# Modulation loaded in two column halves, three layer-1 products split along their rows, memory loaded first

## The chip, the cores and the metric

The kernel runs on one core of one Trainium2 chip. TensorE (PE in the rows) multiplies matrices, VectorE (DVE), ScalarE (ACT) and GpSimd (POOL) work element by element, and SyncE (SP) issues most of the transfers from HBM into SBUF. The metric is the device time of one execution in microseconds, the median of several runs. Lower is better.

## What is computed

Three layers over 256 tokens of width 2048, all in float32. Layer 1, cut to what the change touches:

```
mod = silu(c) @ w_ada + b_ada                       # w_ada: 2048 x 6144
shift, scale, gate = split(mod, 3)
h = rms_norm(x, norm_gain) * (1 + scale) + shift
q_sb, k_sb, v_sb, z_sb, q_r, k_r, v_r, z_r = split(h @ w_in, 8)
oa = stick_breaking_attention(rms_norm(q_sb), rms_norm(k_sb), v_sb) * silu(z_sb)
ob = head_group_norm(retention(rotary(q_r), rotary(k_r), v_r)) * silu(z_r)
x  = x + gate * (concat(oa, ob) @ w_out)
```

Layers 2 and 3 attend, among much else, to a memory of 256 rows: `mem_n = rms_norm(mem)`, and `mem_n @ w_mk`, `mem_n @ w_mv` for each of the two layers. These four memory products depend on nothing of layer 1.

## The kernel before, in words

**Products.** Each product with a weight is a `Gemm`. Its weight comes in chunks of 512 KB (128 partitions x 1024 numbers) into the ring `raw` of `SLOTS` = 6 slots. ScalarE rounds a chunk to `w_hi` (`split_hi`, L364), VectorE computes the rest `w_lo` (`split_lo`, L368), which lies in the same bytes as `raw`, and TensorE multiplies with both (L431 and L432, or L425 to L427 where tokens are the rows of the result). The inputs are kept as a high and a low part too (`xA`). SP issues the load of chunk n once TensorE has used up chunk n - 6 (`chunk_used`, L360). ScalarE and VectorE walk through the chunks with `run_split`: at step i they split chunk i + 3 (`AHEAD` = 3), and before and behind the split they run the small steps of whatever else is under way ("hooks" at positions p, two to a chunk; an odd p comes behind the split). Every engine works through its own list in the order in which it is written; nothing is reordered.

**Order of the products.** `G_MEM` (32 chunks: the four memory products), then `G_SBQK` (q_sb, k_sb, 32 chunks), `G_SBV` (16), `G_RTQK` (32), `G_RTV` (16), `G_SBZ` (16), `G_RTZ` (16), `G_OUT`. The attention of the stick-breaking heads runs in the hooks of `G_RTQK` (`sb_hook`, four units of 8 chunks), the retention in those of `G_SBZ` and `G_RTZ` (`rt_hook`, four units of 8 chunks).

**Modulation.** `silu(c) @ w_ada` is computed on VectorE: GpSimd loads 1 MB pieces of `w_ada` (128 rows of one third) into `ada_ring` (4 slots, L518), VectorE multiplies each by its scalar and adds it to `ada_sum` (L1062), and TensorE adds up the partitions at the end (`ada_columns`, L1629). The 32 pieces of shift and scale are used up during the memory norm and `G_MEM`, the 16 of gate during `G_SBQK` and `G_SBV`, one in four and one in two chunks.

**The start.** SP issues `vec`, `con`, `memT` (2 MB), `xT` (2 MB), and then weights; GpSimd issues the first pieces of `w_ada` beside them. ScalarE squares the memory (L579), TensorE adds the squares over the features (L1615), ScalarE forms the inverse root (L597, L600), and VectorE and ScalarE normalise 16 tiles (L1003, L606, L1009) with `ada` pieces in between. Behind `G_MEM` stand the columns of shift and scale, and then norm 1 of all 16 tiles of x; `G_SBQK` starts with the first four tiles.

## Time and profile before

| | us |
|---|---|
| median of 3 runs (1883.63 to 1887.93) | 1885.12 |
| the profiled execution | 1890.45 |
| its span, first to last instruction | 1888.6 |
| TensorE busy in the span | 1784.2 (94%) |
| VectorE busy | 1235.9 (65%) |
| ScalarE busy | 902.7 (48%) |

In the rows below, a product instruction's line says which kind it is, "idle before <-releaser" says how long the engine had been idle and what ended it, and PEclk is the granted TensorE clock (1.00 is 2.4 GHz, 0.5 is 1.2 GHz). A stage's end is read from the first instruction of the next one.

### The profile page before, as it was taken

To read this page: it belongs to the slowest core of one execution; us is meant where nothing else is said; L and a number is where in the kernel's file an instruction comes from. 1 tells how busy PE (TensorE), PEld (TensorE's weight loads), DVE (VectorE), ACT (ScalarE), POOL (GpSimd) and SP (SyncE) were. 2 spreads that over 40 slices of the span, in tenths; PEclk is the share of its full clock that TensorE was granted. 3 is DMA by queue.
4 is the path that set the end of the run, shared out by engine and by line. 5 is a ranking of instruction groups with operands and counts; after the bars stand their busy time and mean duration, and the time that the engine had idled before them with its cause. 6 is when DMAs were issued, how large, how long until landed. Compare 5 with 4: busy or idle time off the path is not lost.

```text
span 1888.6 us, 23572 instructions
## 1 busy us (share of the span) xinstructions
PE 1784.2 (94%) x9703; PEld 1517.6 (80%) x9703; DVE 1235.9 (65%) x1520; ACT 902.7 (48%) x1158; POOL 75.7 (4%) x87
## 2 busy tenths in 40 slices
PE   1699999999999989999999999999989999999897
PEld 1577888888887878888888888788878888878786
DVE  3978767655477655788567766865464667566754
ACT  2333544454356434666344565644354555455632
POOL 0111000000000000011000000000000000000010
PEclk9798999999999999999999999999989999999999
DMA  8897888556444546666654555565546565444463
GB/s 304 328 350 294 296 290 298 153 148 177 135 145 141 190 149 169 188 189 180 178 145 138 153 167 162 167 191 185 187 141 178 162 194 146 123 123 123 134 187 115
DMA packets 304874, 350.51 MB, mean 186 GB/s; under 512 B 10416, under 2 KB 286000, under 8 KB 298624
## 3 DMA queue, kind: packets, MB, share of 16 engines
q1 hardware_dynamic: 297744, 298.34, 52.5%
q0 software_dynamic: 7024, 50.66, 6.9%
q8 instruction: 78, 1.28, 0.3%
q14 instruction: 28, 0.23, 0.0%
HBM read 346.87 MB, written 2.10 MB: 185 GB/s over the span
## 4 chain that ended last, share of the span: by engine, by line
PE 90%; DVE 5%; DMA 2%; ACT 2%; issue 2%; SPq 0%; DVEq 0%
PE psG L431 48%; PE psG L432 24%; PE psG L425 3%; PE psG L426 3%; PE psG L427 3%; DVE ada_sum L1062 1%; DMA P<-in_memT 1%; PE psH L1615 1%; DMA raw<-in_mem_w 1%; PE psH L1604 1%; DVE w_lo L368 1%; PE psH L1629 1%; DVE W L1003 1%; ACT w_hi L364 1%; PE psH L1890 1%
## 5 line engine op out<-in xcount | busy, mean ns | idle before, releaser
L431 PE MATMUL psG<-xA,w_hi 128*128 128x512 f32 x3520 | 1281.8, 407 | 53.4 <-issue 24.4
L432 PE MATMUL psG<-xA,w_lo 128*128 128x256 f32 x3520 | 994.7, 283 | 0.0
L368 DVE TENSOR_TENSOR w_lo<-raw,w_hi 128x1024 fp32r<-128x1024 f32 (+1 forms) x560 | 686.5, 1239 | 356.9 <-ACT w_hi L364 355.4
L431 PEld LDWEIGHTS psG<-xA,w_hi 128*128 128x128 f32 x3520 | 670.0, 190 | 226.5 <-issue 50.1
L364 ACT ACTIVATE w_hi<-raw 128x1024 fp32r<-128x1024 f32 (+1 forms) x560 | 572.9, 1045 | 372.2 <-DMA raw<-in_w_out 163.9
L432 PEld LDWEIGHTS psG<-xA,w_lo 128*128 128x128 f32 x3520 | 673.7, 191 | 4.4 <-issue 3.8
L400 ACT ACTIVATE P<-psG 128x512 f32<-128x512 f32 x102 | 60.6, 594 | 217.5 <-PE psG L432 217.4
L1033 DVE TENSOR_TENSOR P<-psG,P 128x512 f32<-128x512 f32 (+2 forms) x103 | 70.4, 683 | 116.4 <-ACT P L400 114.1
L1062 DVE SCALAR_TENSOR_TENSOR ada_sum<-ada_ring,silc,ada_sum 128x2048 f32<-128x2048 f32 x48 | 112.6, 2347 | 3.9 <-DMA ada_ring<-in_w_ada 3.8
L425 PE MATMUL psG<-w_hi,xA 128*128 128x512 f32 x192 | 77.7, 405 | 4.4 <-DVE memkv L1033 3.9
L426 PE MATMUL psG<-w_lo,xA 128*128 128x512 f32 x192 | 76.9, 400 | 0.0
L427 PE MATMUL psG<-w_hi,xA 128*128 128x512 f32 x192 | 76.7, 399 | 0.0
L431 PE MATMUL psG<-xB,w_hi 128*128 128x512 f32 x192 | 67.7, 395 | 0.0
L1615 PE MATMUL psH<-W,con 128*128 128x256 f32 x74 | 21.7, 436 | 35.4 <-ACT W L579 35.4
L432 PE MATMUL psG<-xB,w_lo 128*128 128x256 f32 x192 | 53.8, 280 | 0.0
L544 POOL TENSOR_TENSOR W<-W 128x512 f32<-128x512 f32 x9 | 12.5, 1385 | 1007.8 <-ACT W L579 1007.8
L1040 DVE TENSOR_TENSOR xT<-psG,xT 128x512 f32<-128x512 f32 x32 | 22.1, 692 | 45.1 <-PE psG L432 44.6
L431 PE MATMUL psG<-xQ,w_hi 128*128 128x512 f32 x144 | 50.9, 399 | 0.0
L425 PEld LDWEIGHTS psG<-w_hi,xA 128*128 128x128 f32 x192 | 37.5, 195 | 13.3 <-DVE memkv L1033 4.3
L431 PE MATMUL psG<-xK,w_hi 128*128 128x512 f32 x128 | 47.0, 406 | 0.0
L1615 PEld LDWEIGHTS psH<-W,con 128*128 128x128 f32 x74 | 15.3, 220 | 39.0 <-issue 28.5
L427 PEld LDWEIGHTS psG<-w_hi,xA 128*128 128x128 f32 x192 | 37.3, 194 | 8.1
(291 smaller groups left out, 1492.0 us busy)
## 6 DMA issues: line engine op xcount, KB each, us to landing
raw<-in_w_in SPq DMA_DIRECT2D x360, 512.0 KB, 3.8
raw<-in_w_out SPq DMA_DIRECT2D x128, 512.0 KB, 3.4
ada_ring<-in_w_ada POOLq DMA_DIRECT2D x48, 1024.0 KB, 7.9
raw<-in_mem_w SPq DMA_DIRECT2D x32, 512.0 KB, 9.3
raw<-in_w_uq SPq DMA_DIRECT2D x24, 384.0 KB, 3.3
raw<-in_w_ukv SPq DMA_DIRECT2D x32, 128.0 KB, 2.4
raw<-in_w_ukv SPq DMA_DIRECT2D x16, 256.0 KB, 3.2
P<-in_memT SPq DMA_DIRECT2D x1, 2048.0 KB, 25.6
```

Source lines behind the costliest of these rows:

```text
L364: nc.scalar.activation(slot(w_hi, n), slot(raw, n), ACT.Copy).then_inc(hi_ready, 1)
L368: nc.vector.tensor_tensor(slot(w_lo, n), slot(raw, n), slot(w_hi, n), ALU.subtract).then_inc(lo_ready, 1)
L400: nc.scalar.activation(g.dst(b), product(g, b, 0), ACT.Copy).then_inc(copied, 1)
L425: nc.tensor.matmul(out, x_hi, hi[:, w], start=first, stop=False)
L426: nc.tensor.matmul(out, x_hi, lo[:, w], start=False, stop=False)
L427: last = nc.tensor.matmul(out, x_lo, hi[:, w], start=False, stop=end)
L431: nc.tensor.matmul(psG[:, bank + f, :], hi[:, w], x, start=first, stop=False)
L432: last = nc.tensor.matmul(psG[:, bank + f, S:2 * S], lo[:, w], x[:, 0:S], start=False, stop=end)
L1033: v.tensor_tensor(g.dst(b), product(g, b, 1), g.dst(b), ALU.add).then_inc(features_landed, 1)
L1040: ins = v.tensor_tensor(x, src, x, ALU.add)
L1062: v.scalar_tensor_tensor(out=ada_sum[:, part, :], in0=ada_ring[:, n % ADA_SLOTS, :], scalar=silc[:, k:k + 1], in1=ada_sum[:, part, :], op0 ...
L1615: ins = mm(psH[:, norm_bank(n), 0:S], ones, norm_squares(n, g)[:, j * S:j * S + S], start=g == 0 and j == 0, stop=g == 3 and j == 3)
```

## The change

**Memory first.** `memT` comes in four parts of 512 KB, ahead of `con`; `xT` is issued behind the first eight weight chunks; GpSimd issues no `w_ada` before it has pre-added the squares of the memory (`add_squares(0)`: of three groups in four TensorE then has one matmul instead of four, and of norm 1 likewise).

**Modulation in halves.** Shift and scale are loaded as 512 KB pieces (128 rows, half of a third's columns) into a ring of six slots. The 32 pieces of the first column half are used up in `G_MEM`, the 32 of the second in a new stage. Norm 1 of tiles 0 to 7 needs the first half alone and runs in the last three steps of `G_MEM`; tiles 8 to 15 follow in the last three steps of the new stage.

**Products in two halves.** `G_SBQK0`, `G_RTQK0` and `G_SBV0` (16 + 16 + 8 chunks, the new stage of 40) multiply with the first 1024 rows of the weights, which needs tiles 0 to 7. `G_SBQK`, `G_SBV` and `G_RTQK` then do the other 1024 rows (16 + 8 + 16 chunks) and VectorE adds them to what stands in `P` (`adds`: two instructions of 128x512 for each block of two chunks, L1109). `G_RTQK` now spans two units of `sb_hook`; the other two run in `G_RTV`.

**Gate in the weight ring.** The 32 half pieces of the gate are loaded by SP into `raw` itself, as items between the weights (`ITEMS`): behind every second chunk of `G_SBQK`, `G_SBV`, `G_RTV` and `G_SBZ`, and behind every fourth of `G_RTQK`. Item j takes the slot of item j - 6. The piece behind chunk i is added on VectorE at step i, behind the split of chunk i + 3. The gate's columns on TensorE come in two halves, behind `G_RTQK` and behind `G_SBZ`.

```diff
-ADA_SUM, ADA_RING, FIRST_CON, FIRST_WORK = 16, 32, 64, 72
-ADA_SLOTS = 4
-ADA_FIRST, ADA_BLOCK = 8, 6
-SHIFT_AT = 11
+MEM_RAW, FIRST_CON, FIRST_WORK = 32, 64, 72
+ADA_SUM, ADA_RING, GATE_SUM = 64, (48, 52, 56, 60, 72, 76), 60
+ADA_HALF = 32
+MEM_UNITS, EARLY_UNITS = 32, 40
...
+        self.adds, self.per = adds, per or kt // 2
+        self.copied, self.by_scalar = not adds and bool(dst), not adds and bool(tokens)
...
+        def early(k0):
+
+            return dict(x=lambda k: xA[:, k0 + k, :], ready=lambda tiles: (q["nm_lo"], 16 + k0 + tiles), adds=k0 > 0, per=8)
...
-        G_SBQK = Gemm(KT, 8, columns(w_in, 0), dst=into(SBQ), pair=True, **h1)
-        G_SBV = Gemm(KT, 2, columns(w_in, 2048, 512, 2), cols=512, kk=2, tokens=copy_tokens(SBV), **h1)
-        G_RTQK = Gemm(KT, 8, columns(w_in, 4096), dst=into(RTQ), **h1)
+        G_SBQK0, G_SBQK = (Gemm(8, 8, columns(w_in, 0, row0=k0 * NP), dst=into(SBQ), pair=True, **early(k0)) for k0 in (0, 8))
+        G_RTQK0, G_RTQK = (Gemm(8, 8, columns(w_in, 4096, row0=k0 * NP), dst=into(RTQ), **early(k0)) for k0 in (0, 8))
+        G_SBV0, G_SBV = (Gemm(8, 2, columns(w_in, 2048, 512, 2, row0=k0 * NP), cols=512, kk=2, tokens=copy_tokens(SBV),
+                              **early(k0)) for k0 in (0, 8))
...
-        ORDER = [*G_MEM, G_SBQK, G_SBV, G_RTQK, G_RTV, G_SBZ, G_RTZ, G_OUT,
+        ORDER = [*G_MEM, G_SBQK0, G_RTQK0, G_SBV0, G_SBQK, G_SBV, G_RTQK, G_RTV, G_SBZ, G_RTZ, G_OUT,
...
+        GATE_AT = {G_SBQK: lambda i: i % 2 == 1, G_SBV: lambda i: i % 2 == 1, G_RTQK: lambda i: i % 4 == 3,
+                   G_RTV: lambda i: i % 2 == 1, G_SBZ: lambda i: i % 2 == 1}
+        ITEMS = []
+        for g in ORDER:
+            for i in range(len(g.order)):
+                ITEMS.append(("weight", g.c0 + i))
+                if g in GATE_AT and GATE_AT[g](i):
+                    ITEMS.append(("gate", sum(kind == "gate" for kind, _ in ITEMS)))
+        PLACE, LOADS = {}, []
+        for j, (kind, n) in enumerate(ITEMS):
+            by_tile = kind == "weight" and CHUNKS[n][0].by_tile
+            LOADS.append((LOADS[j - SLOTS] if j >= SLOTS else 0) + (CHUNKS[n][0].kk if by_tile else 1))
+            PLACE[kind, n] = j
+
+        def arrived(eng, kind, n):
+            j = PLACE[kind, n]
+            eng.wait_ge(raw_loaded[j % SLOTS], 16 * LOADS[j])
 
         def landed(eng, g, blocks=None):
...
+            j = PLACE["weight", g.c0]
+            end = PLACE["weight", g.c0 + len(g.order)] if g is not ORDER[-1] else len(ITEMS)
+            for j in range(j, end):
+                kind, n = ITEMS[j]
+                if j >= SLOTS:
+                    before, m = ITEMS[j - SLOTS]
+                    sp.wait_ge(*((chunk_used, m + 1) if before == "weight" else (ada_used, 2 * ADA_HALF + m + 1)))
+                if kind == "gate":
+                    k, half = m_to_gate(n)
+                    sp.dma_start(raw[:, j % SLOTS, :], ada_rows(k, 2, half)).then_inc(raw_loaded[j % SLOTS], 16)
+                    continue
+                _, b, c = CHUNKS[n]
+                src, out = g.src(b, c), low(n, raw).rearrange("p (k n) -> p k n", k=g.kk)
                 if g.by_tile:
                     for k in range(g.kk):
-                        sp.dma_start(out[:, k, :].rearrange("p (h n) -> p h n", n=NP), src[:, k]).then_inc(raw_loaded[n % SLOTS], 16)
+                        sp.dma_start(out[:, k, :].rearrange("p (h n) -> p h n", n=NP), src[:, k]).then_inc(raw_loaded[j % SLOTS], 16)
                 else:
-                    sp.dma_start(out, src).then_inc(raw_loaded[n % SLOTS], 16)
...
+            for g in range(4):
+                sp.dma_start(mem_raw[:, 4 * g:4 * g + 4, :], io["memT"].rearrange("(t p) s -> p t s", p=NP)[:, 4 * g:4 * g + 4, :])\
+                  .then_inc(mem_loaded[g], 16)
...
+                if g is G_MEM[0]:
+                    sp.dma_start(xT[:, :, :], io["xT"].rearrange("(t p) s -> p t s", p=NP)).then_inc(loaded["x"], 16)
                 if g is G_SBQK:
-                    sp.wait_ge(q["nm_ss"], 8)
+                    sp.wait_ge(q["ada_cols"], 2)
...
+            add_squares(0)
+            for m, (half, k, part) in enumerate(ADA_ORDER):
+                slot = m % len(ADA_RING)
+                if m == 20:
+                    add_squares(1)
+                if m >= len(ADA_RING):
+                    pool.wait_ge(ada_used, m + 1 - len(ADA_RING))
...
+                if unit in (6, 8, 11, 13):
+                    act.wait_ge(loaded["x"], 16)
+                    norm_square(1, (6, 8, 11, 13).index(unit), xT)
+                if unit == 18:
+                    norm_inverse_root(1)
+                if unit >= MEM_UNITS - 3:
...
+                if g.tokens:
+                    out, bank = g.tokens(b), set_of(g, b)
+                    v.tensor_tensor(out, psG[:, bank:bank + 2, :], out, ALU.add).then_inc(vector_landed, 1)
...
+                    n = m - 2 * ADA_HALF
+                    k, half = m_to_gate(n)
+                    arrived(dve, "gate", n)
+                    src, out = raw[:, PLACE["gate", n] % SLOTS, :], gate_sum[:, :]
+                    if k == 0 and half:
+                        dve.wait_ge(q["gate_cols"], 1)
+                if k == 0:
+                    v.tensor_scalar(out, src, silc[:, k:k + 1], None, ALU.mult).then_inc(ada_used, 1)
+                else:
+                    dve.wait_ge(ada_used, m - (m < 2 * ADA_HALF))
+                    v.scalar_tensor_tensor(out=out, in0=src, scalar=silc[:, k:k + 1], in1=out, op0=ALU.mult,
+                                           op1=ALU.add).then_inc(ada_used, 1)
...
+            def half_norm(half, step):
+                if step == 0:
+                    modulation(half)
+                    dve.wait_ge(q["nm_rs"], 2)
+                for t in (range(0, 4), range(4, 7), range(7, 10))[step]:
+                    norm_step(1, xT, gs, mod, 8 * half + t, 8 * half, 8 * half + 8)
...
+                        for m in range(done[u], done[u + 1]):
+                            ada_add(ADA_HALF * half + m)
+                        if u >= units - 3:
+                            half_norm(half, u - (units - 3))
...
+            def gate_hook(g, u0=0):
+
+                def hook(b, p):
+                    i = 8 * b + p // 2
+                    if p % 2 and GATE_AT[g](i):
+                        ada_add(2 * ADA_HALF + ITEMS[PLACE["weight", g.c0 + i] + 1][1])
+                return hook
+
...
+            def modulation_columns(half):
+                pe.wait_ge(ada_used, ADA_HALF * (half + 1))
+                ada_columns(ada_sum[:, 0, :], 8 * half, None)
+                ada_columns(ada_sum[:, 1, :], KT + 8 * half, "ada_cols", first=False)
+
+            def gate_columns(half):
+                pe.wait_ge(ada_used, 2 * ADA_HALF + KT * (half + 1))
+                ada_columns(gate_sum[:, :], 32 + 8 * half, "gate_cols")
...
+            pe.wait_ge(q["sb_y"], 2)
+            gate_columns(0)
+            run_products(pe, G_RTV, lambda b, p: sb_hook(2 + b, p))
```

How SP's list stands in the stage of `G_SBV`; `raw` is the ring, `in_w_in` the weights, `in_w_ada` the gate's pieces. Before, where `con_65` are constants of layer 1:

```order
L360 DMA raw<-in_w_in 128x4x256 [waits chunk_used] x32
L505 DMA con_65<-in_con 128x1672 [waits nm_ss]
L360 DMA raw<-in_w_in 128x2x512 [waits chunk_used] x16
L360 DMA raw<-in_w_in 128x4x256 [waits chunk_used] x32
L360 DMA raw<-in_w_in 128x2x512 [waits chunk_used] x16
```

and now, from the second half of `G_SBQK` into that of `G_SBV`:

```order
L394 DMA raw<-in_w_in 128x4x256 [waits chunk_used] x2
L386 DMA raw<-in_w_ada 128x1024 [waits ada_used]
L551 DMA con_72<-in_con 128x1672 [waits ada_cols]
L394 DMA raw<-in_w_in 128x2x512 [waits chunk_used] x2
L386 DMA raw<-in_w_ada 128x1024 [waits ada_used]
L394 DMA raw<-in_w_in 128x2x512 [waits chunk_used] x2
L386 DMA raw<-in_w_ada 128x1024 [waits ada_used]
```

What moved: between each two weight loads stands a load that waits for VectorE's addition of an earlier gate piece.

How VectorE's list stands at the start of `G_SBQK`. Before:

```order
L368 TENSOR_TENSOR w_lo<-raw,w_hi 128x1024 x4
L1062 SCALAR_TENSOR_TENSOR ada_sum<-ada_ring,silc,ada_sum 128x2048
L368 TENSOR_TENSOR w_lo<-raw,w_hi 128x1024 x3
L1033 TENSOR_TENSOR P<-psG,P 128x512
L368 TENSOR_TENSOR w_lo<-raw,w_hi 128x1024
L1062 SCALAR_TENSOR_TENSOR ada_sum<-ada_ring,silc,ada_sum 128x2048
```

and now, in its second half:

```order
L409 TENSOR_TENSOR w_lo<-raw,w_hi 128x1024
L1145 SCALAR_TENSOR_TENSOR gate_sum<-raw,silc,gate_sum 128x1024
L1109 TENSOR_TENSOR P<-psG,P 128x512 x2
L409 TENSOR_TENSOR w_lo<-raw,w_hi 128x1024 x2
L1145 SCALAR_TENSOR_TENSOR gate_sum<-raw,silc,gate_sum 128x1024
L1109 TENSOR_TENSOR P<-psG,P 128x512 x2
```

What moved: an addition of a gate piece stands behind every second split instead of every fourth, and each pair of splits is followed by two additions of products. VectorE's list in `G_MEM`, before:

```order
L368 TENSOR_TENSOR w_lo<-raw,w_hi 128x1024
L1062 SCALAR_TENSOR_TENSOR ada_sum<-ada_ring,silc,ada_sum 128x2048
L368 TENSOR_TENSOR w_lo<-raw,w_hi 128x1024
L1062 SCALAR_TENSOR_TENSOR ada_sum<-ada_ring,silc,ada_sum 128x2048
```

and now:

```order
L409 TENSOR_TENSOR w_lo<-raw,w_hi 128x1024
L1145 SCALAR_TENSOR_TENSOR ada_sum<-ada_ring_70,silc,ada_sum 128x1024
L409 TENSOR_TENSOR w_lo<-raw,w_hi 128x1024
L1145 SCALAR_TENSOR_TENSOR ada_sum<-ada_ring_71,silc,ada_sum 128x1024
```

What moved: each split is followed by half as large a piece.

## Rows read from the trace of the kernel before

**Rows 1.** The page, 40 slices of the span: busy tenths of TensorE

```profile
PE   1699999999999989999999999999989999999897
```

**Rows 2.** Windows: window, length, busy us (instructions) of PE, PEld, DVE, ACT, POOL, PEclk, DMA share, GB/s

```profile
49.60:110.00 60.40, 47.03 (x200) 39.15 (x200) 54.52 (x50) 23.20 (x31) 7.44 (x15) 0.81 0.90 334
110.00:181.30 71.30, 68.26 (x346) 57.55 (x344) 58.52 (x40) 22.81 (x24) 6.08 (x12) 0.95 0.90 336
...
278.00:321.60 43.60, 43.60 (x195) 36.09 (x194) 35.81 (x25) 18.52 (x18) 2.64 (x5) 1.00 0.90 313
321.60:437.00 115.40, 115.40 (x628) 96.19 (x627) 69.41 (x70) 60.37 (x71) 0.00 (x0) 1.00 0.51 149
```

**Rows 3.** Chain of waits, the first 50 us: start, us, what

```profile
1.67 25.62 DMA P<-in_memT
...
28.51 8.74 PE psH L1615 x32
...
37.69 0.42 ACT W L600
```

**Rows 4.** Timeline of TensorE: start, us, instruction, idle before it

```profile
49.63 0.79 PE L431 MATMUL psG<-xA,w_hi 128*128 128x512 f32 x1 [12.39 <-DVE xA L1009]
...
50.43 0.63 PE L431 MATMUL psG<-xA,w_hi 128*128 128x512 f32 x1
...
51.07 0.63 PE L431 MATMUL psG<-xA,w_hi 128*128 128x512 f32 x1
...
55.55 0.43 PE L431 MATMUL psG<-xA,w_hi 128*128 128x512 f32 x1
...
177.33 3.63 PE L1629 MATMUL psH<-con,ada_sum 128*128 128x1 f32 x32
185.58 0.76 PE L431 MATMUL psG<-xA,w_hi 128*128 128x512 f32 x1 [4.62 <-issue]
```

**Rows 5.** GB/s in 40 slices of 0:60 us

```profile
GB/s 0 161 366 305 379 419 422 418 420 421 409 418 408 408 378 349 348 347 348 349 348 347 348 350 348 348 334 60 0 0 0 0 0 104 322 273 87 328 328 317
```

**Rows 6.** Chain of waits, one chunk from its load to TensorE

```profile
110.37 16.71 DMA raw<-in_mem_w
...
127.10 1.07 ACT w_hi L364
...
128.19 1.24 DVE w_lo L368
...
129.56 0.47 PE psG L431
```

**Rows 7.** Weight loads of SP (L360), 330:350 us and then 196:280 us

```profile
DMA to landing us min/median/max: 3.6/3.8/3.9
...
DMA to landing us min/median/max: 3.6/4.7/6.8
```

**Rows 8.** Timeline of VectorE in the memory products

```profile
129.34 2.34 DVE L1062 SCALAR_TENSOR_TENSOR ada_sum<-ada_ring,silc,ada_sum 128x2048 f32<-128x2048 f32 x1
131.60 1.22 DVE L368 TENSOR_TENSOR w_lo<-raw,w_hi 128x1024 fp32r<-128x1024 f32 x1
132.73 2.35 DVE L1062 SCALAR_TENSOR_TENSOR ada_sum<-ada_ring,silc,ada_sum 128x2048 f32<-128x2048 f32 x1
```

**Rows 9.** Groups of instructions by form: GpSimd, whole span; VectorE, 196:520 us

```profile
L544 POOL TENSOR_TENSOR W<-W 128x512 f32<-128x512 f32 x9 | 12.5, 1385 | 1007.8 <-ACT W L579 1007.8
...
L1033 DVE TENSOR_TENSOR P<-psG,P 128x512 f32<-128x512 f32 x18 | 12.4, 687 | 7.7 <-ACT P L400 7.7
...
L1134 DVE SCALAR_TENSOR_TENSOR work<-work 128x768 f32<-128x768 f32 x4 | 3.8, 952 | 0.0
```

**Rows 10.** Chain of waits, 196:700: first matmuls of two units of each kind

```profile
325.95 0.86 PE psH L1659 x2
...
354.65 0.86 PE psH L1659 x2
...
516.77 0.86 PE psH L1696 x2
...
545.16 0.86 PE psH L1696 x2
```

326 lines of the change are left out of this document (167 added, 159 removed).

## The prediction

> **What bounds the kernel now.** I read the page's slices first: TensorE is busy nine tenths or more nearly everywhere except in the first two slices [rows 1]. So the end is set by TensorE's work plus its idle time. The windows by stage say where that idle time is: the memory products take 49.6 to 181.3 us with TensorE busy 47.0 of 60.4 and 68.3 of 71.3 us at clocks of 0.81 and 0.95, while from 278 to 437 us it is never idle [rows 2]. The chain of waits gives the cause of the first 50 us: the memory's 2 MB land 25.6 us after their issue, since 4 MB of `w_ada` move beside them, and the inverse root is ready at 38.1 [rows 3]. Two facts shape what follows. At the start, anything that brings the memory earlier moves everything. Behind 278 us there is next to no idle time to win, so each wait that the change adds there costs in full.
>
> Three prices first. A chunk of the token kind takes TensorE 43.6 / 16 = 2.73 us [rows 2]. A unit of `sb_hook` takes 28.7 us (354.65 - 325.95) and one of `rt_hook` 28.4 (545.16 - 516.77) [rows 10]; with the unit's own matmuls at about 6.2 us, eight feature chunks take some 22.4, so 2.8 each. In `G_RTV`, with chunks of 2.73, an `sb_hook` unit would take 28.1 if nothing waits.
>
> **Part 1, the start: 22 us won.** The four memory parts and `con` are alone on the queue until GpSimd starts with `w_ada`. SP's queue alone moves 348 GB/s (the flat stretch from 22 us on, while VectorE takes no piece of `w_ada`) [rows 5], so 0.52 MB takes 1.5 us, and from the first issue at about 1.2 us and a landing time of 3.8 us for one such load [rows 7] the parts land at about 5.2, 6.7, 8.2 and 9.7 us and `con`, which TensorE needs, at 11.2. GpSimd's pre-addition is new here: 1.4 us for 128x512 [rows 9] and between 0.7 and 1.4 for the half, say 0.9: 2.3 a group. Groups 2 and 3 reuse the buffers of 0 and 1, so the third is squared at 11.8 to 12.9, pre-added by 15.3, and TensorE ends with it and four matmuls (16 took 8.74 us with their waits [rows 3], so 0.5 each at most) at 17.7; the root takes 0.8 more and is ready at 18.5 instead of 38.1. Then the same steps as before up to the first product, which took 49.63 - 38.1 = 11.5 us, less one `ada` addition of 2.26 [rows 3, 4, 8]: 9.3. First product at 27.8 instead of 49.6. Bounds: 25 (no queueing) to 32 (the memory slowed by the weights behind it).
>
> **Part 2, the memory products and norm 1: 37 us won, less 8.5.** `G_SBQK`'s 32 chunks ended at 278.0; 32 x 2.8 = 89.6 before that is 188.4, so measured this way the stage took 188.4 - 49.6 = 138.8 us, with the gap in front of 185.58 and the slow clock behind it [rows 2, 4] in it. Bare work is 16 x 2.8 + 16 x 2.73 = 88.5, the slow clock at the start 2.7 (pairs 0.64 us apart instead of 0.35 until 55.5 [rows 4]), seven sum matmuls 3.0, and columns twice 3.8 (3.63 and the step behind it [rows 4]): 101.8. VectorE's step falls from 1.14 + 2.26 = 3.4 us [rows 8] to 1.14 + 1.13 = 2.3, below the chunk's 2.8; TensorE has three split chunks (8.4 us) in hand while norm 1 begins, whose first four tiles took 4.3 us (181.3 to 185.58 [rows 4]); with two splits between them 6.6, so `G_SBQK0` starts without a gap. So the gain is 37.0, and 58.8 with part 1.
> What stalls remain? The DMA engines were 90% busy at 335 GB/s [rows 2]. Now a step needs 0.52 + 0.52 MB: at 348 GB/s for weights alone and at most 420 with pieces of `w_ada` beside them [rows 5] this is 2.5 to 3.0 us, a tie with TensorE's 2.8. And `xT` stands ahead of chunk 8: 2.1 + 0.5 MB at 348 GB/s is 7.5 us from about 47, so chunk 8 is ready at 58 instead of 53. I take 5.5 for it and 3 for the tie; bounds 2 and 22. The stage of 40 chunks has no extra load and no norm in front; I count 0 for it, its stalls being in the bound.
> Net of parts 1 and 2: -50.3.
>
> **Part 3, the gate in the weight ring: 71 us lost.** This is the term that decides. Take three items in a row: chunk, chunk, gate. Six slots hold four chunks and two gate pieces. Gate piece i + 4 takes the slot of gate piece i, and chunk i + 5 is issued behind it on SP. SP waits for `ada_used` of piece i, so chunk i + 5 cannot be issued before that addition either, although its own slot is free. The addition of piece i + 2 stands on VectorE behind the split of chunk i + 5. This closes a loop that has nothing of TensorE in it: addition i -> issue of two loads -> landing of chunk i + 5 -> `w_hi` -> `w_lo` -> addition i + 2. Its length, per two chunks:
> - two loads of 0.52 MB in one queue: 3.8 us for the first [rows 7], and the second 1.5 behind [rows 5], 5.2 with the issue overlapped,
> - landing to `w_lo` starting: 0.02 + 1.07 + 0.02 [rows 6],
> - the split 1.14 and the addition 1.17, half of 2.34 [rows 8], and 0.1 for the semaphore.
> Together 8.7 us, where TensorE needs 5.5 to 5.6. Bounds: 7.2 if the gate piece's transfer cost nothing, 9.5 if the landing is 4.7 as in 196 to 280 us [rows 7].
> - `G_SBQK` and `G_SBV`, 24 chunks. The first addition is at step 1, 10.1 us after the stage's start (chunk 4 is issued as chunk 0 ends, at 2.8, and split 6.2 later, then the addition). Chunk 6 is ready at 17.8 instead of 16.8, and each two chunks take 8.7 from there on: chunk 24, the first of `G_RTQK`, starts at 17.8 + 9 x 8.65 = 95.6 instead of 66.6. Cost 29.
> - `G_RTQK` has a piece behind every fourth chunk, no closed loop, and its units are 28.7 long: 0. But its last addition stands in front of the columns of the gate, where TensorE waits for it: `w_lo` with a load issued four chunks back, a copy of 0.7, and the addition: 4 (bounds 2 and 5).
> - `G_RTV`, two units: four loops of 8.65 = 34.6 and, inside the loop, L1134 at 0.95 and the copy of 128x512 at 0.7 [rows 9]: 36.2 against 28.1, twice: 16.
> - `G_SBZ`, two units: 34.6 and inside it three instructions of the rotary step (two of 128x512 and one of 128x1024, 2.6) and three more of 0.7 to 1.0, 5.1 together: 39.7 against 28.4, twice: 22.
> Sum 71. With 7.2 for the loop it is 34; with 9.5, 91.
> The pages know both pieces of this. The Trainium skill ("DMA: Bandwidth & Descriptors", "Anatomy of one DMA") says that DMA engines never wait on semaphores and that the wait is done by the sequencer that issues, before dispatch. By that rule an SP that waits for a gate piece holds back the weight behind it, which speaks against this change; the trace of before shows no such wait, since its loads of `w_ada` are on GpSimd. The Trainium skill ("SBUF — State Buffer", "The DMA setup-cost knee") gives a load 2 us plus its bytes at 436 GB/s; by this, as an estimate, one load lands after 3.2 us and two in a queue after 4.4, the loop is 7.9, and part 3 costs about 51 and the time is about 1886. The rows show 3.8 for one load, so I keep 8.65.
>
> **Covered.** VectorE's 36 product additions (687 ns each [rows 9], 25 us) lie in the loop's wait for the load, or in `G_RTQK` where VectorE was 60% busy (69.4 of 115.4 us [rows 2]) and comes to about 80%. Without that cover `G_RTQK`'s 16 blocks' worth would cost up to 6.
>
> **Sum.** -58.8 + 8.5 + 71 = +20.7. The profiled execution is 1890.45, which would become 1911; against the median of 1885.12, which is what counts, 1905.8.
>
> **The rivals.**
> - *Short loop* (0.16). The loop closes, but at 7.2 to 7.6 us because two loads of one queue overlap almost fully; the small steps of the heads hide in it. For it: the queue has bandwidth left there (149 GB/s in 321 to 437 us [rows 2]). Against it: 0.5 MB needs 1.5 us at the queue's own rate. Part 3 costs 34 to 42, the time is 1869 to 1877, faster. It is decided at 8.0: below it the gain of the start outweighs the loop.
> - *No loop* (0.07). The gate pieces do not hold the weights back, for instance because VectorE runs its steps far ahead of TensorE. Then only the start counts: 1885.1 - 50.3 + 6 = 1841. Against it: the loop has no step of TensorE, so running ahead gains nothing after the first lap.
> - *Loop and starved start* (0.12). Loads are as slow as in 0 to 180 us, where one took 16.7 us [rows 6]; the tie in the memory products is lost (22 instead of 8.5): 1919.
> - *Cold TensorE* (0.10). Idle gaps of 3 us in each lap make its clock fall as it did behind the gap of 4.6 [rows 4]: chunks of 5 us, and 10 to 20 more: 1916 to 1926.
> Forecast (0.55): 1892 to 1920.
>
> **Numbers.** 1906. The range 1866 to 1926 leaves out "no loop" and the tails of the others. Faster by more than 0.2% (about what a measurement of this kernel can tell from no change): 0.16 + 0.07 + 0.02 = 0.25; the same 0.08; slower 0.67.
>
> **What would show it.** The first product at 25 to 32 us; `G_MEM` over at 127 to 145; in the second halves VectorE's `gate_sum` additions 8 to 9 us apart, with the time in front of the split of chunk i + 5 ended by ScalarE, and ScalarE's ended by the load; SP idle on VectorE's addition; TensorE idle some 3 us for every two chunks of `G_SBQK` and `G_SBV` and not idle in `G_RTQK`. If the additions are 5.6 us apart, part 3 is wrong; if the first product is later than 35 us, part 1 is.

## The result, and the profile after

The changed kernel takes 1966.72 us (median of 4 runs, 1962.0 to 1968.8) against 1886.53 (4 runs, 1883.63 to 1891.14): ratio 1.042, 95% interval 1.039 to 1.045. The forecast was 1906, range 1866 to 1926. The sign was right, and the loss is 80 us instead of 21. The profiled execution took 1965.76, its span is 1963.9.

The page of the changed kernel, 40 slices of 49 us; beside [rows 1] TensorE is now idle in the slices that were full, and its clock is lower there:

```profile
PE   5799987788778998999999999999989999999897
...
PEclk8899998899988999999999999999989999999898
...
L405 ACT ACTIVATE w_hi<-raw 128x1024 fp32r<-128x1024 f32 (+1 forms) x560 | 574.7, 1045 | 493.3 <-DMA raw<-in_w_in 282.5
```

The last line says that ScalarE's splits waited 282.5 us for weight loads alone.

Windows of the changed kernel (window, length, busy us of PE, PEld, DVE, ACT, POOL, PEclk, DMA share, GB/s). The first begins with the first product. The second ends four microseconds before the second halves begin, which is at 263.05; the second half of `G_SBQK` lasts until 332.2 and that of `G_SBV` until 367.0, so the third and fourth window hold most of these two, and then come `G_RTQK` (until 441.3), `G_RTV` (until 520.8) and `G_SBZ` (until 617.1):

```profile
31.10:140.00 108.90, 96.88 (x471) 81.26 (x472) 91.10 (x97) 45.49 (x57) 27.63 (x38) 0.92 0.88 314
140.00:259.00 119.00, 119.00 (x648) 102.45 (x647) 102.59 (x110) 55.83 (x67) 13.78 (x26) 0.98 0.86 292
259.00:334.90 75.90, 59.41 (x281) 49.49 (x280) 38.82 (x45) 19.17 (x20) 0.00 (x0) 0.89 0.57 182
334.90:370.00 35.10, 25.95 (x100) 20.24 (x99) 16.65 (x15) 8.46 (x8) 0.00 (x0) 0.89 0.47 157
370.00:441.30 71.30, 62.75 (x321) 52.04 (x320) 48.59 (x53) 30.43 (x34) 0.00 (x0) 0.93 0.56 176
441.30:520.00 78.70, 64.92 (x249) 49.93 (x249) 37.54 (x37) 27.66 (x29) 0.00 (x0) 0.90 0.50 154
520.00:617.00 97.00, 69.59 (x320) 55.23 (x320) 48.77 (x50) 31.78 (x38) 12.41 (x6) 0.88 0.44 135
```

Two things are to be seen. In no window behind 259 us is any engine or the DMA (share 0.44 to 0.57) full, and yet TensorE is idle 75 of 358 us. That is the mark of a loop of waits. The 119 us ahead of it are full.

TensorE's timeline, the first products of the second half of `G_SBQK` and of `G_RTQK`:

```profile
263.05 0.39 PE L475 MATMUL psG<-xA,w_hi 128*128 128x512 f32 x1
...
367.02 0.77 PE L475 MATMUL psG<-xA,w_hi 128*128 128x512 f32 x1 [3.76 <-DVE w_lo L409]
```

One lap of that loop, in the chain of waits of the changed kernel (start, us, what):

```profile
300.24 1.29 DVE gate_sum L1145
...
301.54 0.34 SPq L386
...
301.93 5.25 DMA raw<-in_w_in
...
307.20 1.07 ACT w_hi L405
...
308.29 0.04 DVE w_lo L409
308.33 1.11 issue
309.43 1.29 DVE gate_sum L1145
...
310.74 0.34 SPq L386
```

VectorE adds a gate piece; SP, which waited for that, issues the next piece (L386) and then a weight; this weight lands, is split by ScalarE and VectorE ("issue" is the rest of the split, 1.15 in all), and only then does VectorE come to its next addition. TensorE is nowhere in it. A lap is 309.43 - 300.24 = 9.19 us, for two chunks.

At the start, the chain of waits of the changed kernel beside [rows 3], then TensorE's timeline:

```profile
3.31 8.41 DMA con<-in_con
...
16.34 4.65 PE psH L1720 x10
21.02 0.39 ACT W L637
...
47.08 17.91 DMA raw<-in_mem_w
```

```profile
31.10 0.80 PE L475 MATMUL psG<-xM,w_hi 128*128 128x512 f32 x1 [10.12 <-DVE xM L1067]
```

The first product is at 31.10 instead of 49.63. A weight issued behind `xT` (SP issued that at 39.0) took 17.91 us to land.

### The profile page after: what moved, and what is told of

It reads as the page before. It is cut to its first block, busy times and chain, and to the rows that moved or that the text cites. A ratio compares the mean times of both kernels' runs of the same rounds, so it can differ in the third digit from the quotient of the medians.

```text
span 1963.9 us, 23699 instructions
## 1 busy us (share of the span) xinstructions
PE 1808.8 (92%) x9667; PEld 1531.2 (78%) x9667; DVE 1260.0 (64%) x1604; ACT 904.1 (46%) x1158; POOL 101.3 (5%) x114
## 3 DMA queue, kind: packets, MB, share of 16 engines
q8 instruction: 78, 1.28, 0.3%
## 4 chain that ended last, share of the span: by engine, by line
PE 77%; DMA 8%; DVE 6%; ACT 5%; issue 3%; SPq 0%; POOL 0%; DVEq 0%; ACTq 0%
PE psG L475 42%; PE psG L476 21%; DMA raw<-in_w_in 7%; ACT w_hi L405 3%; PE psG L469 2%; PE psG L471 2%; PE psG L470 2%; DVE w_lo L409 2%; DVE gate_sum L1145 1%; PE psH L1720 1%; DMA raw<-in_mem_w 1%; PE psH L1734 1%; PE psH L1709 1%; PE psH L2014 1%; PE psH L2015 1%
## 5 line engine op out<-in xcount | busy, mean ns | idle before, releaser
L475 PE MATMUL psG<-xA,w_hi 128*128 128x512 f32 x3392 | 1237.4, 407 | 44.7 <-issue 19.7
L476 PE MATMUL psG<-xA,w_lo 128*128 128x256 f32 x3392 | 960.7, 283 | 0.0
L475 PEld LDWEIGHTS psG<-xA,w_hi 128*128 128x128 f32 x3392 | 649.6, 192 | 210.2 <-issue 37.1
L405 ACT ACTIVATE w_hi<-raw 128x1024 fp32r<-128x1024 f32 (+1 forms) x560 | 574.7, 1045 | 493.3 <-DMA raw<-in_w_in 282.5
L476 PEld LDWEIGHTS psG<-xA,w_lo 128*128 128x128 f32 x3392 | 653.4, 193 | 4.2 <-issue 3.6
L1098 DVE TENSOR_TENSOR P<-psG,P 128x512 f32<-128x512 f32 (+2 forms) x103 | 70.3, 683 | 106.8 <-ACT P L444 104.6
L1145 DVE SCALAR_TENSOR_TENSOR ada_sum<-ada_ring,silc,ada_sum 128x1024 f32<-128x1024 f32 x60 | 79.5, 1330 | 0.0
L469 PE MATMUL psG<-w_hi,xA 128*128 128x512 f32 x128 | 55.6, 435 | 8.9 <-DVE w_lo L409 5.4
L475 PE MATMUL psG<-xM,w_hi 128*128 128x512 f32 x128 | 47.0, 410 | 11.1 <-DVE xM L1067 10.1
L470 PE MATMUL psG<-w_lo,xA 128*128 128x512 f32 x128 | 52.9, 413 | 0.0
L471 PE MATMUL psG<-w_hi,xA 128*128 128x512 f32 x128 | 52.5, 410 | 0.0
L1109 DVE TENSOR_TENSOR xT<-psG,xT 128x512 f32<-128x512 f32 x32 | 22.1, 692 | 44.5 <-PE psG L476 44.0
L1720 PE MATMUL psH<-W,con 128*128 128x256 f32 x70 | 26.0, 511 | 23.3 <-DMA con<-in_con 11.8
L577 POOL DMA_DIRECT2D ada_ring<-in_w_ada x64 | 34.1, 533 | 169.6 <-DVE ada_sum L1145 129.0
L475 PEld LDWEIGHTS psG<-xB,w_hi 128*128 128x128 f32 x192 | 36.0, 187 | 8.3
```

The costliest lines, as they stand in the source:

```text
L405: nc.scalar.activation(high(n), low(n, raw), ACT.Copy).then_inc(hi_ready, 1)
L469: nc.tensor.matmul(out, x_hi, hi[:, w], start=first, stop=False)
L470: nc.tensor.matmul(out, x_hi, lo[:, w], start=False, stop=False)
L471: last = nc.tensor.matmul(out, x_lo, hi[:, w], start=False, stop=end)
L475: nc.tensor.matmul(psG[:, bank + f, :], hi[:, w], x, start=first, stop=False)
L476: last = nc.tensor.matmul(psG[:, bank + f, S:2 * S], lo[:, w], x[:, 0:S], start=False, stop=end)
```

## The experiments

Each kernel was compared with runs of the kernel before on the same chip (medians 1888.8, 1887.1 and 1888.2 us for the three groups of experiments). The theory under test is the closed loop; its rivals are that the additional bytes and additions cost by themselves, and that TensorE's clock, which falls in the gaps, does.

**The addition ahead of the split.** One condition changes; loads, slots and arithmetic stay.

```diff
-                    if p % 2 and GATE_AT[g](i):
+                    if p % 2 == 0 and GATE_AT[g](i):
```

> The changed kernel with one edit: VectorE adds a gate piece ahead of the split of chunk i+3 in the same step, instead of behind it. Same loads, same order on SP's queue, same arithmetic. Theory (closed loop): the addition no longer stands behind w_lo of the chunk whose load its own predecessor released, so the loop of 9.2 us per two chunks opens; the stages G_SBQK to G_SBZ go at TensorE's pace, gate_sum additions 5.6 us apart in the second halves, and nearly all of the 120 us that these stages lost comes back: 1840 to 1865 us. Rival (bytes): the second load of 0.52 MB per step and the added VectorE work set the pace, whatever the order: 1955 to 1970, additions still 9 apart. Rival (cold TensorE by itself): 1930 to 1970.

Measured: 1911.64 us, 55 less than the changed kernel, and 47 to 72 more than expected. So the order of two VectorE instructions carries 55 us, and something else is left: the expected "nearly all" of the loss did not come back. The mean distance of the additions in the first 11 laps fell from 9.29 to 6.8 us ((343.0 - 268.1) / 11), not to 5.6. In the chain of waits of this kernel the addition still stands once in the way, but no longer in every lap:

```profile
295.22 5.42 DMA raw<-in_w_in
300.66 1.07 ACT w_hi L405
301.76 1.23 DVE w_lo L409
302.98 0.61 DVE P L1109
...
304.23 1.22 DVE w_lo L409
305.44 1.21 DVE gate_sum L1145
306.67 0.34 SPq L386
```

**No gate pieces at all.** `GATE_AT` is left unused and `gate_sum` is zero, so this kernel leaves the gate's third of `w_ada` out.

> The changed kernel without any gate pieces: the gate's third of w_ada is neither loaded nor added (gate_sum is set to zero), the rest is as changed. This gives the change's start alone. Theory (closed loop): 1835 to 1855, since the start gained 40 us and part 3 costs all the rest. Rival (something else in the second halves costs time, for instance split accumulation or the product additions on VectorE): 1880 to 1960, and G_RTQK, G_RTV and G_SBZ are still longer than before. The difference to the kernel with the addition ahead of the split is what gate pieces cost when they close no loop: 5 to 15 us.

Measured: 1853.85 us, as the theory said. But the difference to the kernel with the addition ahead of the split is 57.8 us, not 5 to 15: gate pieces cost that much although the loop is open. The windows of this kernel from 252 us (its second halves begin at 261.4) to the gate's first columns and from there to its second columns are full, nearly at full clock. The second halves of `G_SBQK` and `G_SBV` take 67.0 us for 24 chunks where the prediction counted 66.6. So the split products and their additions in `P` cost next to nothing:

```profile
252.00:386.80 134.80, 134.03 (x700) 112.59 (x699) 90.78 (x107) 58.89 (x65) 0.00 (x0) 0.99 0.57 172
386.80:505.20 118.40, 117.44 (x583) 95.07 (x583) 70.18 (x72) 57.83 (x68) 8.69 (x6) 1.00 0.48 142
```

**A longer lap.**

```diff
-                        ada_add(2 * ADA_HALF + ITEMS[PLACE["weight", g.c0 + i] + 1][1])
+                        n = ITEMS[PLACE["weight", g.c0 + i] + 1][1]
+                        if n % KT:
+                            dve.wait_ge(ada_used, 2 * ADA_HALF + n)
+                            link(v.tensor_scalar(gate_sum[:, :], gate_sum[:, :], 1.0, None, ALU.mult))
+                        ada_add(2 * ADA_HALF + n)
```

> The changed kernel with one more VectorE instruction ahead of each addition of a gate piece but the first of a half (gate_sum times 1.0, 128x1024, about 0.7 to 1.1 us, waited for). Theory (closed loop): VectorE's time is a term of the loop, so each of the about 28 laps in G_SBQK, G_SBV, G_RTV and G_SBZ grows by that amount, 9.2 to about 10.1 us: +20 to +30, 1987 to 1997. Rival (SP's queue or the bytes set the pace, VectorE has slack, since it is busy 64%): +0 to +5.

Measured: 1994.47 us, +27.75. These are the instruction's rows:

```profile
L1203 DVE TENSOR_SCALAR gate_sum<-gate_sum x30: 684/686/689, 284.7 to 636.6; 128x1024 f32<-128x1024 f32 x30
L1145 DVE SCALAR_TENSOR_TENSOR gate_sum<-raw,silc,gate_sum x30: 1283/1285/2193, 285.4 to 637.3; 128x1024 f32<-128x1024 f32 x30
```

30 of them at 0.69 us are 21 us, and the first addition of all came 3.6 us later than in the changed kernel (275.6 instead of 272.0) ahead of any of them. So all of it reached the end, and the 3 us that these two leave are within the spreads (1962.0 to 1968.8 and 1992.3 to 1998.3). Over the first 11 laps the distance is 10.0 instead of 9.29. VectorE is busy 64% of the span, and yet each of its microseconds in the lap is paid for.

**The same instruction with the loop open.** Both edits together.

> Both edits together: the addition of a gate piece ahead of the split (1911.6 us by itself) and one more VectorE instruction of 686 ns ahead of each addition (which cost +27.7 us in the changed kernel). Theory (closed loop): with the addition ahead of the split the loop is open, so the same 30 instructions now lie mostly beside other work: 1911 to 1920. Rival (VectorE's time costs wherever it stands in these stages): +20 to +28 again, 1931 to 1940.

Measured: 1917.17 us, +5.5 over the addition ahead alone, with overlapping spreads (1906.5 to 1925.2 against 1907.1 to 1915.1). The same 30 instructions cost 27.75 inside the loop and 5.5, not clear of noise, outside. This pair shows the loop best: nothing but the place differs.

**Four slots for weights, and no pieces.**

```diff
                 kind, n = ITEMS[j]
-                if j >= SLOTS:
-                    before, m = ITEMS[j - SLOTS]
-                    sp.wait_ge(*((chunk_used, m + 1) if before == "weight" else (ada_used, 2 * ADA_HALF + m + 1)))
                 if kind == "gate":
-                    k, half = m_to_gate(n)
-                    sp.dma_start(raw[:, j % SLOTS, :], ada_rows(k, 2, half)).then_inc(raw_loaded[j % SLOTS], 16)
                     continue
+                if j >= SLOTS and ITEMS[j - SLOTS][0] == "weight":
+                    sp.wait_ge(chunk_used, ITEMS[j - SLOTS][1] + 1)
...
```

> No gate piece is loaded or added (gate_sum is zero: the gate's third of w_ada is left out), but the slots of the ring that the pieces took stay empty, so weights keep only four of six slots in the stages from G_SBQK to G_SBZ. With all six slots and no pieces the time was 1853.85 us; with the pieces in these slots and added ahead of the split 1911.6. Theory (the ring is too short): of these 58 us most are the four slots: a slot comes free when its chunk is used, then 3.8 to 5.4 us of load, 1.07 of w_hi, 1.23 of w_lo and up to 1.4 of product additions on VectorE are 8 to 9 us, and TensorE has three chunks, 8.4 us, in hand: 1880 to 1905. Rival (bytes and additions): the second load per two chunks and its 1.28 us on VectorE are the cost; without them 1855 to 1862.

Measured: 1899.98 us, 46 more than with six slots. This is a cost that the forecast lacked: two gate pieces in six slots leave four for weights. The traces of the two kernels say where it falls: `G_SBQK` with `G_SBV` takes 70.8 us instead of 67.0 and `G_RTQK` 62.5 instead of 60.2, but `G_RTV` takes 76.7 instead of 57.6 and `G_SBZ` 74.5 instead of 59.2. So four slots nearly suffice for a slot's turn (load, two splits, product additions in front), and fall short where the heads' small steps come on top of it. ScalarE's waits for weights in the same stretch (engine, line, waited for: us, times, longest) of this kernel, then of the one with six slots:

```profile
ACT w_hi L402 <- DMA raw<-in_w_in: 135.4, 61, 8.0
```

```profile
ACT w_hi L405 <- DMA raw<-in_w_in: 48.1, 30, 2.9
```

**Slots of their own.**

```diff
+        gate_ring = [sb(f"gate_ring{i}", [NP, D_MODEL // 2], place=in_p(t)) for i, t in enumerate((56, 24, 28, 16, 20))]
...
+        GATE_PLACE = [(2, 0, 1)[n % 3] for n in range(26)] + [2, 3, 4, 0, 3, 4]
...
-                if kind == "gate":
-                    k, half = m_to_gate(n)
-                    sp.dma_start(raw[:, j % SLOTS, :], ada_rows(k, 2, half)).then_inc(raw_loaded[j % SLOTS], 16)
-                    continue
...
+                    sp.wait_ge(ada_used, 2 * ADA_HALF + last + 1)
+                    k, half = m_to_gate(m)
+                    sp.dma_start(gate_ring[place][:, :], ada_rows(k, 2, half)).then_inc(gate_loaded[place], 16)
```

> The changed kernel with the gate pieces in slots of their own (three, then five places of P that are free at the time) instead of in the weight ring; weights have all six slots. Same bytes, same queue and place in SP's order, additions behind the split as in the changed kernel, SP waits for a piece three back. Theory (it is the shared slots, as a closed loop and as a shortage): 1855 to 1870 us, additions 5.6 us apart, i.e. no-pieces 1853.85 plus what 32 loads and additions cost beside other work. Rival (bytes on SP's queue, VectorE's 41 us of additions): 1890 to 1960.

Measured: 1868.15 us, 98.6 less than the changed kernel with the same bytes, the same additions behind the split and the same queue, and ratio 0.990 (0.988 to 0.992) to the kernel before. The rival of bytes and additions is refuted: they cost 1868.15 - 1853.85 = 14.3 us, not 113. The additions of the first 11 laps are 5.5 us apart, TensorE's pace, as expected. The gate's additions keep their size (the row of this kernel), and end at 513.7 instead of 612.8:

```profile
L1155 DVE SCALAR_TENSOR_TENSOR gate_sum<-gate_ring,silc,gate_sum x30: 1274/1278/1282, 275.1 to 513.7; 128x1024 f32<-128x1024 f32 x30
```

**Small pieces in the loop.** Slots and waits are as in the changed kernel; each piece is an eighth as wide and is added eight times over, so the gate's values are not the reference's.

```diff
-                    sp.dma_start(raw[:, j % SLOTS, :], ada_rows(k, 2, half)).then_inc(raw_loaded[j % SLOTS], 16)
+                    sp.dma_start(raw[:, j % SLOTS, 0:NP], ada_rows(k, 2, half)[:, 0:NP]).then_inc(raw_loaded[j % SLOTS], 16)
...
```

> The changed kernel with gate pieces of 128 columns instead of 1024 (64 KB instead of 512 KB); VectorE adds these 128 columns eight times over, so its instruction stays as wide and the gate's values are not the reference's (seven eighths of the gate's third of w_ada are left out). Slots, waits and order are as in the changed kernel. Theory (the weight behind the piece lands 5.25 us after its issue because two loads share the queue): it lands after 3.8 to 4.0, the lap is 7.8 to 8.0 us instead of 9.2 and about 28 laps save 1.3 each, somewhat less where a unit's own steps end last: 1930 to 1948. Rival (short bytes cost nothing, the wait and the landing time of one load make the lap): 1960 to 1967.

Measured: 1949.23 us, a microsecond above the theory's range. The chain of waits of this kernel shows the term as expected, 3.93 instead of 5.25, and a lap of 314.03 - 306.09 = 7.94:

```profile
299.91 3.93 DMA raw<-in_w_in
...
303.86 1.06 ACT w_hi L405
...
306.09 1.29 DVE gate_sum L1146
...
314.03 1.29 DVE gate_sum L1146
```

But the saving of 17.5 us is mostly the 11 laps of 1.3 in `G_SBQK` and `G_SBV` (first addition to twelfth: 102.2 us in the changed kernel, 88.2 here). From the first to the last addition of the second half, in `G_RTV` and `G_SBZ`, it is 161.1 against 155.4, 0.4 a lap: there the waits of the heads' own steps end last in many laps.

**A warm TensorE.** Three matmuls whose result nobody uses stand behind each of 24 chunks.

```diff
+                    for _ in range(3):
+                        mm(psH[:, BA, :], xA[:, 0, 0:NP], xA[:, 0, :], start=True, stop=True)
```

> The changed kernel with three matmuls more (128x512, result unused) behind every chunk of G_SBQK's and G_SBV's second halves: 24 chunks, 72 matmuls, meant to lie in TensorE's gaps and to keep its clock up there. Theory (closed loop without TensorE in it): the stages last as long as VectorE's loop, 9.2 to 9.3 us per two chunks, whatever TensorE's clock; within 3 us of 1966.7, with a granted clock nearer to 1.0 in these stages. Rival (the clock that falls in the gaps adds time of its own): 5 to 15 us faster. If the fillers don't fit the gaps, slower by up to 10.

Measured: 1964.74 us, -2.0, inside the spread of either. The window of this kernel that holds `G_SBQK` and a little of either neighbour has the clock at 0.94 instead of 0.89 and TensorE busy 66.93 instead of 59.41, in the same time:

```profile
259.00:334.90 75.90, 66.93 (x333) 55.19 (x332) 37.78 (x42) 18.68 (x19) 0.00 (x0) 0.94 0.58 186
```

The two stages together last 104.6 us instead of 104.0. So the clock does fall in the gaps, but in these two stages keeping more of it up brings nothing that the times show: TensorE isn't what is waited for. In `G_RTV` and `G_SBZ`, where TensorE's small steps stand between the heads' own, this was not tried.

**The start alone, on the kernel before.** The diff's other half is left away.

```diff
+            for g in range(4):
+                sp.dma_start(mem_raw[:, 4 * g:4 * g + 4, :], ...).then_inc(mem_loaded[g], 16)
             sp.dma_start(con[:, :], io["con"]).then_inc(loaded["con"], 16)
...
+                if n == SLOTS:
+                    sp.dma_start(xT[:, :, :], ...).then_inc(loaded["x"], 16)
...
+            pool.wait_ge(mem_loaded[3], 16)
```

> The kernel before with part 1 alone: the memory in four parts ahead of con, w_ada from GpSimd only when the last of them has landed, xT behind the sixth weight chunk; whole rows, no column halves, gate as before. Theory (start and halves are two separate gains): the root of the memory's norm is ready at 18 to 20 us instead of 38.1, the first product at about 31, and some of the 18 us won is given back since w_ada, which used to arrive in this time, now shares the engines with the weights: 1865 to 1880. Rival (w_ada bounds the first 180 us as a whole: 16 MB of it have to be in before norm 1): nothing won, 1883 to 1890.

Measured: 1870.65 us, ratio 0.991 (0.988 to 0.994). The first product is at 33.47. Some twenty lines win 18.1 us over the kernel before; the whole change wins 18.9 once the gate has slots of its own.

**xT in parts, no pre-additions.** On top of slots of their own.

```diff
+                if n in (6, 8, 10, 12):
+                    x = n // 2 - 3
+                    sp.dma_start(xT[:, 4 * x:4 * x + 4, :], ...).then_inc(mem_loaded[x], 16)
...
-                if g is G_MEM[0]:
-                    sp.dma_start(xT[:, :, :], ...).then_inc(loaded["x"], 16)
...
-                if m == 20:
-                    add_squares(1)
```

> Slots of their own for the gate pieces, and two edits at the memory products: xT in four parts ahead of weight chunks 6, 8, 10 and 12 instead of 2 MB in front of chunk 8, and the squares of norm 1 summed by TensorE (16 matmuls of 256 columns) without GpSimd's pre-additions, beside which VectorE's additions took 2.30 us instead of 1.28. In the trace without gate pieces TensorE was idle 5.2 and 6.4 us in 30 to 60 and 60 to 90 us, and its clock fell to 0.83. Theory (the start is held by the one long load behind 45.7 us and by two engines slowing each other): 8 to 12 us less than with slots of their own alone, 1846 to 1858. Rival (w_ada's and the weights' bytes bound the first 240 us, whatever stands where): within 3 us of it.

Measured: 1858.15 us, 10.0 less; the fastest kernel here that leaves nothing out, ratio 0.985 (0.983 to 0.987) to the kernel before, 108.6 us under the changed one.

**Only the pre-additions taken away.**

> Slots of their own and norm 1 without GpSimd's pre-additions, xT in one piece ahead of chunk 8 as in the changed kernel. It parts the 10 us that both edits won together (1868.15 to 1858.15). Theory A (most of it is xT's place: a weight behind it landed after 17.8 us): 1863 to 1868. Theory B (most is the two engines slowing each other: three additions of 2.30 instead of 1.28 us, three splits of 1.75 instead of 1.23, and TensorE's wait for the pre-additions, 5.0): 1858 to 1863.

Measured: 1866.03 us, -2.1, with overlapping spreads (1862.23 to 1871.36 against 1866.63 to 1870.18): theory A. By the medians `xT`'s place carries about 8 of the 10 us. The traces show 4.5 of it directly: TensorE's wait in front of the second block of products is 7.9 us here and 3.4 with `xT` in parts. Another 3.2 arises in `G_SBV0`, which no edit touches: it took 28.6 us here and 25.4 there, with the clock of 230 to 262 us at 0.89 and at 1.00. So a part of the 8 may not be `xT`'s.

**con second.**

```diff
-            sp.dma_start(con[:, :], io["con"]).then_inc(loaded["con"], 16)
+                if g == 0:
+                    sp.dma_start(con[:, :], io["con"]).then_inc(loaded["con"], 16)
...
-            add_squares(0)
+            pool.wait_ge(mem_loaded[3], 16)
```

> On top of slots of their own, xT in parts and no pre-additions in norm 1: con is loaded second, behind the first quarter of the memory, norm 0 is summed by TensorE alone too, and GpSimd starts with w_ada when the memory's last part has landed. In the trace with xT in parts TensorE waited for con until 11.4 us and ended the sums at 20.6, four GpSimd and TensorE steps behind one another. Theory (the chain con, sums, root sets the first product): sums over at 15 to 17, first product at 26 to 28 instead of 30.8, 1852 to 1856 us against 1858.15. Rival (weights or w_ada, which come later or press harder, set the pace behind it): within 2 us of 1858.

Measured: 1861.55 us, +3.4 with overlapping spreads (1857.0 to 1864.9 against 1855.1 to 1860.3). The theory, 1852 to 1856, was not met; the rival said within 2 us of 1858, and the time is 1.6 above that. The first product did come four microseconds earlier, as computed, and the second block of products started when it had started before. `G_SBQK0` too starts when it did (141.15 and 140.83); what the trace has more behind it, 3.2 us, is in `G_SBV0` again, at a clock of 0.89. TensorE's timeline, of this kernel and then of the one with con behind the memory:

```profile
26.76 0.80 PE L489 MATMUL psG<-xM,w_hi 128*128 128x512 f32 x1 [10.12 <-DVE xM L1078]
49.53 0.47 PE L489 MATMUL psG<-xM,w_hi 128*128 128x512 f32 x1 [0.32 <-DVE w_lo L423]
59.71 0.79 PE L483 MATMUL psG<-w_hi,xM 128*128 128x512 f32 x1 [7.13 <-DVE memkv L1109]
```

```profile
30.78 0.80 PE L489 MATMUL psG<-xM,w_hi 128*128 128x512 f32 x1 [10.12 <-DVE xM L1077]
50.03 0.47 PE L489 MATMUL psG<-xM,w_hi 128*128 128x512 f32 x1 [0.27 <-DVE w_lo L423]
59.94 0.80 PE L483 MATMUL psG<-w_hi,xM 128*128 128x512 f32 x1 [3.36 <-DVE memkv L1108]
```

The idle time went from in front of the first product to in front of the second block, 7.13 instead of 3.36. It is the loads: ScalarE's waits for them between 34 and 62 us (us, times, longest), of this kernel and then of the other, are

```profile
ACT w_hi L419 <- DMA raw<-in_mem_w: 15.4, 4, 11.5
```

```profile
ACT w_hi L419 <- DMA raw<-in_mem_w: 10.9, 4, 6.1
```

**From the changed kernel to no pieces, 112.9 us, in steps**: opening the loop gives 55.1, leaving the pieces out while weights keep four slots 11.7, and the two slots more 46.1. Another way is 98.6 for slots of their own and 14.3 for leaving the pieces out. These are differences between kernels and depend on the order of the steps: no run closes the loop while weights have all six slots. The stages, from the first product instruction of each to that of the next (us, one trace each; "base" is what the prediction counted without the loop):

| stage | base | changed | addition ahead | four slots, no pieces | slots of their own | no pieces |
|---|---|---|---|---|---|---|
| `G_SBQK`, `G_SBV` | 66.6 | 104.0 | 78.4 | 70.8 | 67.0 | 67.0 |
| `G_RTQK` | 57.4 | 74.3 | 68.2 | 62.5 | 63.1 | 60.2 |
| `G_RTV` | 56.2 | 79.5 | 77.3 | 76.7 | 59.2 | 57.6 |
| `G_SBZ` | 56.8 | 96.3 | 75.6 | 74.5 | 63.6 | 59.2 |

## Why the prediction was wrong in size

The prediction's own terms beside the same stretches, from the changed kernel's profile. The base of a stage is the time that the prediction counted for it without the loop.

| term | predicted | measured |
|---|---|---|
| parts 1 and 2, up to the second halves | -50.3 | -36.8 |
| `G_SBQK`, `G_SBV` (24 chunks) | +29 | +37.4 |
| `G_RTQK` and the boundary behind it | +4 | +16.9 |
| `G_RTV` | +16 | +23.3 |
| `G_SBZ` | +22 | +39.5 |
| sum | +20.7 | +80.3 |

For the first row: 188.4 - 50.3 + 32 x 2.8 + 8 x 2.73 = 249.5 was due, and the stage began at 263.05. The others are stage lengths less base: 263.05 to 367.02 less 66.6; to 441.3 less 57.4; to 520.8 less 56.2; to 617.1 less 56.8. That the sum meets the difference of the medians is luck: from trace to trace the first matmul of the third `rt_hook` unit stands at 619.84 instead of 545.16 [rows 10], 74.7 later, and the spans differ by 75.3. The base is too small, since it leaves out the gate's columns, which before were part of `G_RTV` (48.1 us for 16 chunks of 2.73), and the profiled execution of the kernel before was 4 us above the median.

**The start, part 1** (27.8, bounds 25 to 32): 31.1, inside the bounds. `con` landed at 11.72 instead of 11.2 and the sums ended at 21.0, not 17.7: the sums of the groups stood one behind another with ScalarE's and GpSimd's steps between them (4.65 us for the last ten matmuls alone). That the same gain is had without the rest of the change is shown by the start alone. But the value put on this part was too high, since the run with con second won 4 us here and nothing at the end.

**Part 2** (-37.0, stalls 8.5): `xT` ahead of chunk 8 was the suspected place and its size was wrong. A weight behind it landed after 17.91 us where 7.5 were counted. `w_ada` comes in beside it through the other queue; that this is the reason was not tested. TensorE waited 8.8 us for it in front of the second block of products, and 12.0 in all in `G_MEM` where 8.5 were counted. `G_MEM` took 114.5 us (31.1 to 145.6) instead of 98.0 + 8.5; the 4.5 that the waits leave I put down to the slower clock behind them (0.92 over the window, as an estimate; no run parts it). The stage of 40 chunks was counted at nothing, and its window, 119.00 of 119.00, has no idle time; it took 117.5 us instead of 111.4 and the second columns' 3.8, so 2.2 over. With the first product 3.3 late, this is the 13.5 of the first row.

**The closed loop, part 3**, is shown as mechanism. Most of the expected signs are there. In the first 11 laps the additions are 9.29 us apart on the mean where 8 to 9 stood, SP waits on VectorE, and TensorE is idle (75 us). Two are not: `G_MEM` was over at 145.6, just outside 127 to 145, and `G_RTQK`, expected without idle time, has 8.6 us of it. The lap, term by term: the weight behind the piece 5.25 (5.2 predicted), landing to `w_lo` 1.11 (1.11), the split 1.15 (1.14), the addition 1.29 (1.17, as half of 2.34; by these two, and taking the rest as going with the width, some 0.2 us of it does not shrink), and SP's issue with its two semaphores 0.39, which had been called overlapped, where 0.1 stood for the semaphore. That is 9.19; the prediction's terms add up to 8.72, and it counted the laps at 8.65. The 7.9 worked out from the Trainium skill ("SBUF — State Buffer", "The DMA setup-cost knee") was further away: by its figure two loads land after 4.4 us, and here the second took 5.25. The rule of the Trainium skill that the issuing sequencer does the waiting ("DMA: Bandwidth & Descriptors", "Anatomy of one DMA") is what this trace shows: SP's issue, 0.34 us, begins 0.02 us behind each addition.

The longer lap explains the 8.4 us that `G_SBQK` and `G_SBV` lost beyond the forecast (11 laps of 0.64 are 7.1). It does not explain the other 38 by which part 3 missed. **The step that failed is that part 3 priced the loop alone.** "Six slots hold four chunks and two gate pieces" stands in the prediction and was used for the loop only. That four slots are by themselves too few for weights was put at nothing, and the run without pieces in them puts 46 us on it. By the table of stages, 19 of it are in `G_RTV` and 15 in `G_SBZ`, where the heads' small steps find no stock of split chunks to be covered by. In `G_RTV` the 16 us booked on the loop are not its own: opening the loop gives back 2.2, and four slots without any piece cost 19.2 over six. In `G_SBZ` opening the loop gives back 20.7, near the 22 forecast, and the shortage comes on top: two units take 48 us each instead of the 39.7 counted. `G_RTQK`, "no closed loop, 0", lost 13 more than the boundary's 4. By the kernels side by side its 16.9 are 2.8 that it has without pieces too (the gate's columns, which the base leaves out, are most of it), 2.3 for four slots, 5.7 for the pieces with the addition ahead of the split, and 6.1 for the addition behind it. Why the place of the addition matters in a stage with a piece behind every fourth chunk stays open. Without any loop, four slots give 1900 without pieces and 1912 with them: the forecast of 1906 is the time of a kernel that lacks the loop it was built on.

**The rivals.** *Short loop* (7.2 to 7.6): refuted, 9.19. Even with a piece of 64 KB the lap is 7.94. *No loop*, 1841: refuted for the change as it stands; a kernel without the loop and without the pieces took 1853.85, and one with the pieces in slots of their own 1868.15. *Loop and starved start*: its half on the start came true, since the start lost 13.5 of its gain, as much as this case had; its time, 1919, did not. *Cold TensorE*, +10 to +20: the clock did fall, to 0.89, and a kernel that keeps it up in two of the stages is not clearly faster (2.0 us, inside the spreads); in the other stages this was not tried. The range's upper end, 1926, was built from one added case at a time. Loop, slots and start came together, and the tail was not allowed for.

## What to carry to other kernels

Where a second kind of item enters a ring, count two things: the loop through the new item's consumer and the issuing queue, and the slots that the first kind has left against landing time plus everything until the data can be used. An instruction that frees a slot belongs ahead of one that waits for what that slot's successor in the queue brings; the exchange of two instructions was worth 55 us here. When a window shows no engine above nine tenths, follow the chain for one period and add it up; its members are few, and each microsecond in it is paid for even on an engine that is mostly idle. A shortage of slots need not show in every stage: here it cost 4 us in `G_SBQK` and `G_SBV` and 34 in `G_RTV` and `G_SBZ`. And a first product that comes earlier is worth what its supply is worth: ask what is late next before its time is booked.
